# Two attention stages of a three-block layer stack, with heads taken in pairs

## The chip, the cores and the metric

One core of a Trainium2 chip runs the whole program in one launch. The metric is device microseconds for one execution of it. TensorE (PE in the profile), VectorE (DVE), ScalarE (ACT) and the queue of SyncE (SP), which issues the transfers, run side by side and meet at semaphores.

## The reference, cut to what matters

The program computes three transformer-like blocks for 512 tokens of width 1024 in fp32. Two of their pieces are touched, both with 8 heads of width 64:

```python
# block 1: the attention over selected keys (8 heads of 64), queries in 4 blocks of 128
logits = jnp.einsum('bqhd,bqkhd->bqhk', qb, k_sel) * scale
logits = jnp.where(valid[:, :, None, :], logits, -jnp.inf)
p = jax.nn.softmax(logits, axis=-1)
out = jnp.einsum('bqhk,bqkhd->bqhd', p, v_sel)
# block 2: the neighbourhood attention (8 heads of 64), local keys with a bias, and 256 context keys
s_loc = jnp.einsum('brnqhd,brnjwhd->bhrnqjw', qb, k_band) + bias
s_loc = jnp.where(col_valid[:, :, None, :], s_loc, NEG_INF)
s_ctx = jnp.einsum('brnqhd,blhd->bhrnql', qb, kcx)
p = jax.nn.softmax(jnp.concatenate([s_loc, s_ctx], axis=-1), axis=-1)
o = p_loc @ v_band + p_ctx @ vcx
```

The kernel does both densely: the selection of keys and the window are a bias that is added before the softmax.

## The kernel before

The program is a row of stages with a barrier between them. Each stage gives each engine its own list of instructions, written out in Python and never reordered; waits on named counters stand in the lists. `project` (L351) multiplies weight blocks with activations, one tile of 128 output rows after another, and takes other work along in the dictionaries `tensor_beside`, `scalar_beside` and `vector_beside`: a part at key n stands behind tile n, a part at n - 0.5 stands in the middle of tile n on TensorE, and behind tile n - 1 on the two others.

**The selected-key stage** (`dsa_attention`, L1584) runs beside eight such tiles (L454, 8 matmul records of 512 columns each, taken from the bank by VectorE in L1626). **The neighbourhood stage** (`neighbourhood_attention`, L1757) has no tiles: TensorE does attention and two small sums for the normalisation of a convolution (`conv_norm`, L1709), nothing else.

Both use class `Attention` (L1346). Its unit is one head and one block of 128 queries, 32 units a stage. A unit goes through these steps, on one engine after the other:

- scores on TensorE (L1395): one matmul of 64 rows by up to 512 key columns (selected keys: 128, 256, 384 or 512 of them, by the query block), or 512 and 256 columns (neighbourhood). They go to one of two sets of score banks, by turns.
- on VectorE, scale and bias (L1439, counter `softened`) and the row minimum (L1448). In the neighbourhood stage ScalarE scales the 256 context columns (`scale_plain`, L1469, counter `plain_scaled`).
- on ScalarE the exponential with its row sum (L1487), on VectorE the reciprocal (L1454) and the normalisation (L1456).
- on TensorE the transposes (L1410), on ScalarE the copy out of the bank (L1481), on TensorE the products with the values (L1421): a matmul of 128 rows and 64 output columns for each 128 keys, moving 128 columns.

In the neighbourhood stage VectorE adds the window to the bias table of a head before its first unit (L1783), and the queue loads the tables ahead (L1772), two buffers by turns.

The units are staggered. In turn i TensorE does the scores of unit i+1, the transposes of unit i-2 and the values of unit i-3. The scores of unit i wait until unit i-2 has left the same banks. Both operands are fp32, and each fp32 matmul stands in the trace as two records with a weight load each; a transpose is one record.

## Time and profile before

| | |
|---|---|
| median of 3 runs | 3605.81 us (3605.07 to 3607.76) |
| the profiled execution | 3607.01 us, its span 3605.2 us |
| TensorE busy | 3319.2 us, 92% of the span |
| VectorE busy | 1498.6 us, 42% |
| ScalarE busy | 728.0 us, 20% |
| mean granted TensorE clock | 0.964 |

The span is the time between the first and the last instruction in the profile of one execution. A matmul record's length includes the way through the array, so that records which follow each other overlap; what one costs is read from start to start. The granted clock is 1.00 at 2.4 GHz and 0.50 at 1.2 GHz.

### The profile page before, as it was taken

To read this page: it belongs to the slowest core of one execution; us is meant where nothing else is said; L and a number is where in the kernel's file an instruction comes from. 1 tells how busy PE (TensorE), PEld (TensorE's weight loads), DVE (VectorE), ACT (ScalarE), POOL (GpSimd) and SP (SyncE) were. 2 spreads that over 40 slices of the span, in tenths; PEclk is the share of its full clock that TensorE was granted. 3 is DMA by queue.
4 is the path that set the end of the run, shared out by engine and by line. 5 is a ranking of instruction groups with operands and counts; after the bars stand their busy time and mean duration, and the time that the engine had idled before them with its cause. 6 is when DMAs were issued, how large, how long until landed. Compare 5 with 4: busy or idle time off the path is not lost. (4 is left out here: it accounts for less than half of the span.)

```text
span 3605.2 us, 39699 instructions
## 1 busy us (share of the span) xinstructions
PE 3319.2 (92%) x16514; PEld 1917.2 (53%) x16514; DVE 1498.6 (42%) x2289; ACT 728.0 (20%) x1116; POOL 0.2 (0%) x4
## 2 busy tenths in 40 slices
PE   7998999998998969999989898899998999999997
PEld 3485545444455633332323232587554887877874
DVE  2563147611376432212121211436442767466662
ACT  2210232311105310000000000200521323231403
POOL 0000000000000000000000000000000000000000
PEclk9997999999998979999999999999999999999998
DMA  7202042123111049999999999322111212211110
GB/s 254 93 3 71 24 137 103 47 94 140 59 66 36 12 163 387 428 427 428 427 428 428 427 428 427 123 94 88 51 56 61 70 47 70 71 70 47 71 47 24
DMA packets 120306, 588.33 MB, mean 163 GB/s; under 512 B 8896, under 2 KB 11072, under 8 KB 95424
## 3 DMA queue, kind: packets, MB, share of 16 engines
q1 hardware_dynamic: 120128, 585.80, 40.8%
q8 instruction: 131, 2.15, 0.2%
q14 instruction: 47, 0.39, 0.0%
HBM read 583.68 MB, written 2.10 MB: 162 GB/s over the span
## 5 line engine op out<-in xcount | busy, mean ns | idle before, releaser
L454 PE MATMUL ps<-hT,weight_ring 128*128 128x512 f32 x1216 | 544.1, 605 | 28.6 <-ACT hT L593 8.8
L454 PE MATMUL ps<-work,weight_ring 128*128 128x512 f32 (+1 forms) x960 | 425.0, 592 | 18.3 <-PEq L2443 8.3
L454 PEld LDWEIGHTS ps<-hT,weight_ring 128*128 128x128 f32 x1216 | 233.3, 195 | 316.0 <-issue 304.8
L454 PEld LDWEIGHTS ps<-work,weight_ring 128*128 128x128 f32 x960 | 181.0, 194 | 215.6 <-issue 205.0
L2016 PE MATMUL ps<-weight_ring,work 128*64 128x512 f32 x944 | 217.5, 605 | 31.2 <-DMA weight_ring<-in_w_up 17.6
L326 DVE TENSOR_TENSOR work<-work,ps 128x512 f32<-128x512 f32 x196 | 134.7, 687 | 248.7 <-PE ps L441 244.1
L441 PE MATMUL ps<-weight_ring 128*128 128x256 f32 x896 | 202.8, 380 | 0.0
L2145 DVE SCALAR_TENSOR_TENSOR xT<-ps,mod,xT 128x512 f32<-128x512 f32 x128 | 96.1, 751 | 228.3 <-PE ps L2034 225.9
L441 PE MATMUL ps<-hT,weight_ring 128*128 128x256 f32 x704 | 165.4, 393 | 19.5 <-DVE hT L602 15.6
L441 PEld LDWEIGHTS ps<-weight_ring 128*128 128x128 f32 x896 | 170.1, 190 | 24.3 <-issue 1.9
L2016 PE MATMUL ps<-work 128*64 128x512 f32 x688 | 158.2, 603 | 21.6 <-DMA work<-in_w_up 13.5
L441 PE MATMUL ps<-weight_ring,spare_slot 128*128 128x256 f32 x704 | 159.7, 380 | 3.6 <-DVE weight_ring L292 3.6
L2016 PEld LDWEIGHTS ps<-weight_ring,work 128*64 128x64 f32 x944 | 66.2, 138 | 175.9 <-issue 131.3
L441 PEld LDWEIGHTS ps<-hT,weight_ring 128*128 128x128 f32 x704 | 137.3, 197 | 41.6 <-issue 21.8
L441 PEld LDWEIGHTS ps<-weight_ring,spare_slot 128*128 128x128 f32 x704 | 133.4, 190 | 23.3 <-issue 5.8
L1395 PE MATMUL ps<-work 64*128 64x256 f32 (+5 forms) x256 | 106.0, 521 | 20.1 <-DVE work L1439 13.0
L2016 PEld LDWEIGHTS ps<-work 128*64 128x64 f32 x688 | 48.1, 138 | 125.6 <-issue 95.4
L2140 DVE TENSOR_TENSOR work<-work,ps 128x512 f32<-128x512 f32 x32 | 33.9, 1060 | 191.6 <-PE ps L2016 191.0
L2160 DVE COPY work<-ps 128x512 f32<-128x512 f32 x16 | 11.1, 692 | 243.4 <-PE ps L2070 243.4
L545 ACT COPY work<-ps 128x512 f32<-128x512 f32 (+1 forms) x45 | 24.6, 547 | 397.1 <-PE ps L454 208.3
L2070 PE MATMUL ps<-weight_ring,work 128*64 128x512 f32 x448 | 100.2, 595 | 4.0 <-DMA weight_ring<-in_w_down 2.3
L1421 PE MATMUL ps<-work 128*64 128x128 f32 (+1 forms) x704 | 99.8, 285 | 0.0
(346 smaller groups left out, 4169.8 us busy)
## 6 DMA issues: line engine op xcount, KB each, us to landing
weight_ring<-in_w_gate SPq DMA_DIRECT2D x34, 2048.0 KB, 40.2
weight_ring<-in_w_down SPq DMA_DIRECT2D x28, 2048.0 KB, 40.3
weight_ring<-in_w_up SPq DMA_DIRECT2D x25, 2048.0 KB, 38.2
work<-in_w_up SPq DMA_DIRECT2D x23, 2048.0 KB, 38.2
work<-in_w_gate SPq DMA_DIRECT2D x20, 2048.0 KB, 40.2
work<-in_w_down SPq DMA_DIRECT2D x20, 2048.0 KB, 40.3
weight_ring<-in_w_in_odd SPq DMA_DIRECT2D x20, 2048.0 KB, 7.8
weight_ring<-in_w_in SPq DMA_DIRECT2D x18, 2048.0 KB, 9.0
```

The costliest lines, as they stand in the source:

```text
L326: v(dve.tensor_tensor(out, x, got, op), sig if out is steps[-1][0] else None)
L441: ins = pe.matmul(bank[:, j * L:(j + 1) * L], st, mv, start=k == 0, stop=k == 3)
L454: ins = pe.matmul(bank[0:m, 0:f], w[:, k, where:where + m], src[:, k, 0:ntok], start=k == 0, stop=k == kt - 1)
L545: return (lambda a, act, ps, sig: a(act.copy(out, ps), sig), None)
L1395: ins = pe.matmul(self.score_banks(i)[:, c0:c0 + n], u["q"], k, start=True, stop=True)
L1421: ins = pe.matmul(self.ch.ps[u["rows"], self.value_bank + gi % 2, u["col"]:u["col"] + P], val, self.pT[(i - 3) % 2][:, t * P:(t + 1) * P], ...
L2016: ins = pe.matmul(ps[64 * h:64 * h + 64, 1 + 2 * u + n, :], xs[:, 2 * (i % 2) + t, i // 2, :], w[:, t, c0:c0 + 512], start=i == 0 and t == ...
L2070: ins = pe.matmul(ps[64 * q:64 * q + 64, 7, :], hidT[:, i // 2, t, i % 2, :], w[:, t, q * 512:(q + 1) * 512], start=i == 0 and t == 0, sto ...
L2140: v(dve.tensor_tensor(by_tile(hid[:, p, :]), strided(sil[:, p, :]), strided(ps[:, 3 + p, :]), MUL), hid_ready)
L2145: v(dve.scalar_tensor_tensor(ch.xT[:, n, :], ps[:, scatter_banks(e, i // 2)[i % 2], :], ch.mod2[:, 40 + n, 0:1], ch.xT[:, n, :], MUL, ADD) ...
L2160: v(dve.tensor_copy(y, ps[:, 7, :]), y_ready)
```

## The change

A new class `PairAttention` takes the place of `Attention` in the two stages (a third user of `Attention`, in block 3, stays). Its unit is a pair of heads and one block of queries, 16 pairs a stage. The two heads of a pair have their queries and keys in rows 0 to 63 and 64 to 127 of the array, and the score matmuls of the two are written alternately. The values of the two heads go to output columns 0 to 63 and 64 to 127 of one bank, again written alternately. The four sets of banks stay in number: what were two sets of score banks for consecutive units is now one set, half of it for each head of the pair. So the scores of pair i+1 wait until pair i has left the banks. In turn i TensorE does the scores of pair i+1, the transposes of the first head of pair i-2, the values of pair i-3, and the transposes of the second head of pair i-2. Six probability buffers and four for the transposed ones take room in the spare slot. The bias tables have four buffers in the place of `hT`, and VectorE prepares two of them at a time. The convolution's parts stand behind turns 0, 1, 2, 3 and 5 instead of 0, 1, 3, 5 and 8.

```diff
@@ -1494,6 +1494,158 @@
...
+class PairAttention:
+        self.turn_bank, self.value_bank = bank + 2 * width, bank + 3 * width
+        pieces = [x[:, n:n + cols] for x in rooms for n in range(0, SLOT - cols + 1, cols)]
+        self.S, self.pT = pieces[0:6], pieces[6:10]
...
+    def score_banks(self, a):
+        b = self.bank + self.width * a
+        return self.ch.ps[:, b:b + self.width, :].rearrange("p b n -> p (b n)")
...
+    def score(self, pe, i):
+        if i < self.N:
+            u = self.pairs[i]
+            if i >= 1:
+                pe.wait_ge(self.softened.sem, self.softened.at(2 * i))
+                if u["plain"]:
+                    pe.wait_ge(self.plain_scaled.sem, self.plain_scaled.at(2 * i))
+            for c0, n in u["keys"]:
+                for a in range(2):
+                    ins = pe.matmul(self.score_banks(a)[:, c0:c0 + n], u["q"][a], u["k"][a][:, c0:c0 + n], start=True,
+                                    stop=True)
+            ins.then_inc(self.scores.sem, 1)
+            self.scores.total += 1
+    def turn(self, pe, i, a):
+        if 0 <= i < self.N:
+            pe.wait_ge(self.normed.sem, self.normed.at(2 * i + a + 1))
+            if 2 * i + a >= 1:
+                pe.wait_ge(self.copied.sem, self.copied.at(2 * i + a))
+            for t in range(self.pairs[i]["cols"] // P):
+                ins = pe.transpose(self.turn_banks()[:, t * P:(t + 1) * P],
+                                   self.S[2 * (i % 3) + a][:, t * P:(t + 1) * P], self.ch.m("ident"))
+            ins.then_inc(self.turned.sem, 1)
+            self.turned.total += 1
+    def values(self, pe, i):
+        if 0 <= i < self.N:
+            u, g = self.pairs[i], self.group[i]
+            pe.wait_ge(self.copied.sem, self.copied.at(2 * i + 2))
+            if g >= 2:
+                pe.wait_ge(self.taken.sem, self.taken.at(g - 1))
+            n = len(u["v"][0])
+            for t in range(n):
+                for a in range(2):
+                    ins = pe.matmul(self.ch.ps[64 * a:64 * a + 64, self.value_bank + g % 2, u["col"]:u["col"] + P],
+                                    u["v"][a][t], self.pT[2 * (i % 2) + a][:, t * P:(t + 1) * P], start=t == 0,
+                                    stop=t == n - 1)
+            ins.then_inc(self.summed.sem, 1)
+            self.summed.total += 1
+    def tensor(self, i):
+        def part(pe):
+            if i == 0:
+                self.score(pe, 0)
+            self.score(pe, i + 1)
+            self.turn(pe, i - 2, 0)
+            self.values(pe, i - 3)
+            self.turn(pe, i - 2, 1)
+        return part
+    def vector(self, i):
+        def part(v, dve):
+            if i < self.N:
+                u = self.pairs[i]
+                v.after(self.scores, i + 1)
+                if i >= 3:
+                    v.after(self.turned, 2 * (i - 2))
+                if u.get("prepare"):
+                    u["prepare"](v, dve)
+                for a in range(2):
+                    b, w = u["bias"][a], u["biased"]
+                    v(dve.scalar_tensor_tensor(self.S[2 * (i % 3) + a][:, 0:w], self.score_banks(a)[:, 0:w], -self.scale, b,
+                                               MUL, SUB), self.softened)
+                for a in range(2):
+                    if u["plain"]:
+                        v.after(self.plain_scaled, 2 * i + a + 1)
+                    v(dve.tensor_reduce(self.st[:, 2 * (i % 3) + a, 1:2], self.S[2 * (i % 3) + a][:, 0:u["cols"]], AXX, MIN),
+                      self.taken_max)
+            if 1 <= i < self.N + 1:
+                j = i - 1
+                for a in range(2):
+                    stat, x = self.st[:, 2 * (j % 3) + a, :], self.S[2 * (j % 3) + a][:, 0:self.pairs[j]["cols"]]
+                    v.after(self.expd, 2 * j + a + 1)
+                    v(dve.reciprocal(stat[:, 3:4], stat[:, 2:3]))
+                    v(dve.tensor_scalar(x, x, stat[:, 3:4], None, MUL), self.normed)
+            if i >= 5 and self.pairs[i - 5]["close"] is not None:
+                v.after(self.summed, i - 4)
+                self.pairs[i - 5]["close"](v, dve, self.ch.ps[:, self.value_bank + self.group[i - 5] % 2, :], self.taken)
+        return part
+    def scale_plain(self, act_line, act, i):
+        if i < self.N and self.pairs[i]["plain"]:
+            act_line.after(self.scores, i + 1)
+            if i >= 3:
+                act_line.after(self.turned, 2 * (i - 2))
+            c0, w = self.pairs[i]["plain"]
+            for a in range(2):
+                act_line(act.mul(self.S[2 * (i % 3) + a][:, c0:c0 + w], self.score_banks(a)[:, c0:c0 + w], -self.scale),
+                         self.plain_scaled)
+    def scalar(self, i):
+        def part(line, act):
+            if i == 0:
+                self.scale_plain(line, act, 0)
+            for a in range(2):
+                j = i - 2
+                if 0 <= j < self.N:
+                    n = self.pairs[j]["cols"]
+                    line.after(self.turned, 2 * j + a + 1)
+                    if j >= 2:
+                        line.after(self.summed, j - 1)
+                    line(act.copy(self.pT[2 * (j % 2) + a][:, 0:n], self.turn_banks()[:, 0:n]), self.copied)
+                if i < self.N:
+                    x, stat = self.S[2 * (i % 3) + a][:, 0:self.pairs[i]["cols"]], self.st[:, 2 * (i % 3) + a, :]
+                    line.after(self.taken_max, 2 * i + a + 1)
+                    line(act.activation(x, x, ACT.Exp, bias=stat[:, 1:2], scale=-1.0, accum_out=stat[:, 2:3]), self.expd)
+            self.scale_plain(line, act, i + 1)
+        return part
+    def spread(self, beside, places):
+        for i in range(self.turns):
+            beside.add(places[min(i, len(places) - 1)], self.tensor(i), self.scalar(i), self.vector(i))
...
@@ in dsa_attention
...
     q, k, v, gate, bias, out = (ch.slot(9), ch.slot(10), ch.slot(4), ch.slot(3), ch.slot(7), ch.slot(11))
-    units = []
-    for h in range(8):
-        rows, j = slice(64 * (h % 2), 64 * (h % 2) + 64), h // 2
+    pairs, both = [], (slice(0, 64), slice(64, 128))
+    for j in range(4):
         for s in range(4):
             n = P * (s + 1)
             def close(line, dve, ps, sig, j=j):
                 line(dve.tensor_tensor(out[:, j, :], ps, gate[:, j, :], MUL), sig)
-            units.append(dict(
-                q=q[rows, j, s * P:(s + 1) * P], keys=[(k[rows, j, 0:n], 0)],
-                biases=[(bias[:, s, 0:n], 0, n)], plain=[], cols=n,
-                values=[v[:, t, h * HD:(h + 1) * HD] for t in range(s + 1)],
-                rows=rows, col=s * P, close=close if h % 2 == 1 and s == 3 else None))
+            pairs.append(dict(
+                q=[q[rows, j, s * P:(s + 1) * P] for rows in both], k=[k[rows, j, 0:n] for rows in both], keys=[(0, n)],
+                bias=[bias[:, s, 0:n]] * 2, biased=n, plain=None, cols=n,
+                v=[[v[:, t, (2 * j + a) * HD:(2 * j + a + 1) * HD] for t in range(s + 1)] for a in range(2)],
+                col=s * P, close=close if s == 3 else None))
     beside = Beside()
-    att = Attention(ch, units, HD ** -0.5, bank=3, width=1, room=ch.slot(0, 2))
-    att.spread(beside, [-1] * 3 + sorted(halves(0, 8) * 2))
+    att = PairAttention(ch, pairs, HD ** -0.5, 3, 1, [ch.slot(0, 2).rearrange("p k t -> p (k t)"), ch.spare[:, :]], T)
+    att.spread(beside, [-1] * 2 + halves(0, 8))
     beside.project(ch, 2, tiles, banks=3)
@@ in neighbourhood_attention
-    flat = ch.slot(11).rearrange("p a t -> p (a t)")
-    tab = [flat[:, i * 896:(i + 1) * 896] for i in range(2)]
+    flat = ch.hT[:, :, :].rearrange("p k t -> p (k t)")
+    tab = [flat[:, i * 896:(i + 1) * 896] for i in range(4)]
     loaded = ch.counter("bias_loaded")
 
     def load(sp):
         softened = att.softened
         for h in range(8):
-            if h >= 2:
-                sp.wait_ge(softened.sem, softened.at(4 * (h - 1)))
-            sp.dma_start(tab[h % 2], ch.A["rpb"][:, h * 896:(h + 1) * 896]).then_inc(loaded.sem, 16)
+            if h >= 4:
+                sp.wait_ge(softened.sem, softened.at(8 * (h // 2 - 1)))
+            sp.dma_start(tab[h % 4], ch.A["rpb"][:, h * 896:(h + 1) * 896]).then_inc(loaded.sem, 16)
             loaded.total += 16
             sp.wait_ge(loaded.sem, loaded.total)
 
-    units = []
-    for h in range(8):
-        rows, j = slice(64 * (h % 2), 64 * (h % 2) + 64), h // 2
-
-        def prepare(line, dve, h=h):
-            line.after(loaded, 16 * (h + 1))
-            t = tab[h % 2].rearrange("p (r c) -> p r c", c=64)
-            line(dve.tensor_tensor(t, t, ch.m("win")[:, 0:64].unsqueeze(1).to_broadcast([P, 14, 64]), ADD))
+    pairs, both = [], (slice(0, 64), slice(64, 128))
+    for j in range(4):
+        def prepare(line, dve, j=j):
+            for h in (2 * j, 2 * j + 1):
+                line.after(loaded, 16 * (h + 1))
+                t = tab[h % 4].rearrange("p (r c) -> p r c", c=64)
+                line(dve.tensor_tensor(t, t, ch.m("win")[:, 0:64].unsqueeze(1).to_broadcast([P, 14, 64]), ADD))
+        def close(line, dve, ps, sig, j=j):
+            line(dve.tensor_copy(out[:, j, :], ps), sig)
         for s in range(4):
-            def close(line, dve, ps, sig, j=j):
-                line(dve.tensor_copy(out[:, j, :], ps), sig)
-            units.append(dict(
-                q=q[rows, j, s * P:(s + 1) * P], keys=[(k[rows, j, 0:512], 0), (k[rows, j, 512:768], 512)],
-                biases=[(tab[h % 2][:, (6 - 2 * s) * 64:(6 - 2 * s) * 64 + 512], 0, 512)], plain=[(512, 256)],
-                cols=768, values=[v[:, t, h * HD:(h + 1) * HD] for t in range(6)],
-                rows=rows, col=s * P, close=close if h % 2 == 1 and s == 3 else None,
-                prepare=prepare if s == 0 else None))
-    att = Attention(ch, units, HD ** -0.5, bank=0, width=2, room=ch.slot(9, 2))
+            c0 = (6 - 2 * s) * 64
+            pairs.append(dict(
+                q=[q[rows, j, s * P:(s + 1) * P] for rows in both], k=[k[rows, j, :] for rows in both],
+                keys=[(0, 512), (512, 256)], bias=[tab[(2 * j + a) % 4][:, c0:c0 + 512] for a in range(2)], biased=512,
+                plain=(512, 256), cols=768,
+                v=[[v[:, t, (2 * j + a) * HD:(2 * j + a + 1) * HD] for t in range(6)] for a in range(2)],
+                col=s * P, close=close if s == 3 else None, prepare=prepare if s == 0 else None))
+    att = PairAttention(ch, pairs, HD ** -0.5, 0, 2, [ch.slot(9, 2).rearrange("p k t -> p (k t)"), ch.spare[:, :]], 768)
     (total, square_total), (square, take_root, finish), (centre, scale), made = conv_norm(
         ch, y, ch.slot(5), ch.slot(6), 7)
 
     def conv_made(pe):
         pe.wait_ge(made.sem, made.at(4))
-    convolution = {0: (total, None, centre), 1: (None, square, None), 3: (square_total, take_root, scale),
-                   5: (None, finish, None), 8: (conv_made, None, None)}
+    convolution = {0: (total, None, centre), 1: (None, square, None), 2: (square_total, take_root, scale),
+                   3: (None, finish, None), 5: (conv_made, None, None)}
     beside = Beside()
     for i in range(att.turns):
         beside.add(-1, att.tensor(i), att.scalar(i), att.vector(i))
```

**The neighbourhood stage, TensorE.** The list of one turn in its middle, before (L1395 scores, L1410 transposes, L1421 values; one unit):

```order
L1395 MATMUL ps<-work 128x512 [waits plain_scaled,scores_scaled]
L1395 MATMUL ps<-work 128x256
L1410 MATMUL ps<-masks,work 128x128 [waits probs_copied,probs_normed]
L1410 MATMUL ps<-masks,work 128x128 x5
L1421 MATMUL ps<-work 64x128 [waits probs_copied]
L1421 MATMUL ps<-work 64x128 x5
```

The same list after, one turn again, which is two heads (L1542 scores, L1553 transposes, L1567 values):

```order
L1542 MATMUL ps<-work 128x512 [waits plain_scaled,scores_scaled]
L1542 MATMUL ps<-work 128x512
L1542 MATMUL ps<-work 128x256 x2
L1553 MATMUL ps<-masks,work 128x128 [waits probs_copied,probs_normed]
L1553 MATMUL ps<-masks,work 128x128 x5
L1567 MATMUL ps<-spare_slot,work 64x128 [waits probs_copied]
L1567 MATMUL ps<-spare_slot,work 64x128 x11
L1553 MATMUL ps<-masks,spare_slot 128x128 [waits probs_copied,probs_normed]
L1553 MATMUL ps<-masks,spare_slot 128x128 x5
```

The number of matmuls for a head is as before; the matmuls of the two heads now stand next to each other, and the second head's transposes stand behind the values.

**The neighbourhood stage, ScalarE.** One turn before (L1481 the copy of transposed probabilities, L1487 the exponential, L1469 the context columns of the next unit):

```order
L1481 COPY work<-ps 128x768 [waits values_summed,probs_turned,plain_scaled]
L1487 ACTIVATE work,small<-work,small 128x768 [waits maxima_ready,probs_copied]
L1469 ACTIVATE work<-ps 128x256 [waits probs_turned,scores,exps_done]
```

And one turn after (L1635 the copy, L1639 the exponential, L1621 the context columns of the next pair):

```order
L1635 COPY spare_slot<-ps 128x768 [waits values_summed,probs_turned,plain_scaled]
L1639 ACTIVATE work,small<-work,small 128x768 [waits maxima_ready,probs_copied]
L1635 COPY spare_slot<-ps 128x768 [waits values_summed,probs_turned,exps_done]
L1639 ACTIVATE spare_slot,small<-spare_slot,small 128x768 [waits maxima_ready,probs_copied]
L1621 ACTIVATE work<-ps 128x256 [waits probs_turned,scores,exps_done]
L1621 ACTIVATE work<-ps 128x256 [waits plain_scaled]
```

The context columns of both heads of the next pair now stand behind the copy and the exponential of the second head.

**The selected-key stage, VectorE.** The list from the end of a tile on, after (L1777 takes the tile's bank, L1594 is scale and bias, L1599 the minimum, L1606 and L1607 the normalisation):

```order
L1777 TENSOR_TENSOR work<-ps,work 128x512 [waits tile_ready,probs_normed]
L1594 SCALAR_TENSOR_TENSOR work<-ps,work 128x512 [waits probs_turned,scores,tile_vector_done]
L1594 SCALAR_TENSOR_TENSOR work<-ps,work 128x512 [waits scores_scaled]
L1599 TENSOR_REDUCE small<-work 128x1 [waits scores_scaled]
L1599 TENSOR_REDUCE small<-work 128x1 [waits maxima_ready]
L1606 RECIPROCAL small<-small 128x1 [waits exps_done,maxima_ready]
L1607 TENSOR_SCALAR work<-work,small 128x384 [waits vector_step]
```

The pair's scale and bias stand behind the tile's L1777, as a unit's stood before; TensorE's next scores, right behind the tile's last matmul in its list, now wait for these two L1594 instead of for those of a unit earlier.

## Rows read from the trace of the kernel before

**Rows 1.** Windows of the stages: us, then busy (x records) by engine, clock, DMA, GB/s.

```profile
638.00:731.00 93.00, 92.62 (x366) 47.05 (x367) 56.50 (x139) 35.84 (x97) 0.00 (x0) 0.95 0.09 30
1077.00:1231.00 154.00, 140.71 (x720) 93.99 (x720) 95.47 (x149) 84.22 (x143) 0.00 (x0) 0.89 0.12 38
1150.00:1220.00 70.00, 70.00 (x410) 48.25 (x410) 52.59 (x84) 40.88 (x76) 0.00 (x0) 1.00 0.07 21
```

**Rows 2.** Timeline of TensorE, neighbourhood stage: start us, length us, operation.

```profile
1138.77 1.55 PE L1395 MATMUL ps<-work 64*128 64x512 f32 x4
1140.25 0.88 PE L1410 MATMUL ps<-masks,work 128*128 128x128 f32 x6
1141.06 1.52 PE L1421 MATMUL ps<-work 128*64 128x128 f32 x12
1142.51 1.55 PE L1395 MATMUL ps<-work 64*128 64x512 f32 x4
```

**Rows 3.** Timeline of ScalarE and VectorE, neighbourhood stage.

```profile
1130.14 0.93 ACT L1487 ACTIVATE work<-work,small 128x768 f32<-128x768 f32 x1
...
1131.20 0.38 ACT L1469 ACTIVATE work<-ps 128x256 f32<-128x256 f32 x1
...
1131.68 0.95 DVE L1448 TENSOR_REDUCE small<-work 128x1 f32<-128x768 f32 x1 [2.91 <-ACT work L1469]
```

**Rows 4.** Groups by line, 1130 to 1225 us: busy us, mean ns, idle before.

```profile
L1448 DVE TENSOR_REDUCE small<-work 128x1 f32<-128x768 f32 x25 | 23.8, 953 | 23.4 <-ACT work L1469 23.0
...
L1481 ACT COPY work<-ps 128x768 f32<-128x768 f32 x25 | 20.0, 799 | 36.0 <-PE ps L1410 36.0
...
L1439 DVE SCALAR_TENSOR_TENSOR work<-ps,work 128x512 f32<-128x512 f32 x24 | 16.6, 692 | 0.8
...
L1783 DVE TENSOR_TENSOR work<-work,masks 128x896 f32<-128x896 f32 x6 | 6.6, 1093 | 0.5 <-PE ps L1410 0.4
```

**Rows 5.** Timeline of TensorE where other stages alternate halves or quarters.

```profile
205.54 3.73 PE L1007 MATMUL ps<-work 64*64 64x128 f32 x128 [2.22 <-PEq L936]
...
1357.14 5.38 PE L2016 MATMUL ps<-weight_ring,work 128*64 128x512 f32 x24
...
1459.19 1.13 PE L2034 MATMUL ps<-work 64*128 64x512 f32 x4
```

**Rows 6.** Timeline of TensorE behind pauses; the pause stands in brackets.

```profile
1086.42 1.80 PE L1395 MATMUL ps<-work 64*128 64x512 f32 x4 [2.72 <-DVE work L1439]
...
1116.48 2.92 PE L1395 MATMUL ps<-work 64*128 64x512 f32 x4 [5.14 <-DVE work L1439]
...
2835.21 4.96 PE L441 MATMUL ps<-spare_slot,weight_ring 128*128 128x256 f32 x14 [2.40 <-DVE work L326]
...
3007.64 3.72 PE L441 MATMUL ps<-spare_slot,weight_ring 128*128 128x256 f32 x16 [2.40 <-DVE work L326]
```

**Rows 7.** Windows behind such pauses; the clock is third from the end.

```profile
2835.00:2838.50 3.50, 3.29 (x8) 2.67 (x9) 3.39 (x4) 0.83 (x2) 0.00 (x0) 0.53 0.40 147
...
3007.00:3011.00 4.00, 3.36 (x16) 2.98 (x17) 3.89 (x4) 0.91 (x2) 0.00 (x0) 1.00 0.48 178
1087.60:1104.60 17.00, 13.46 (x36) 7.86 (x35) 10.54 (x17) 10.88 (x19) 0.00 (x0) 0.50 0.10 28
```

**Rows 8.** The bias tables (L1772) and timeline of the start-up.

```profile
DMA to landing us min/median/max: 3.3/3.6/7.3
...
1084.55 1.09 DVE L1783 TENSOR_TENSOR work<-work,masks 128x896 f32<-128x896 f32 x1 [20.03 <-DMA work<-in_rpb]
...
1130.63 2.20 PE L1395 MATMUL ps<-work 64*128 64x512 f32 x4
```

**Rows 9.** Timeline of TensorE over one tile, and a group of VectorE, selected-key stage.

```profile
700.97 1.99 PE L454 MATMUL ps<-work,weight_ring 128*128 128x512 f32 x4
702.88 0.48 PE L1395 MATMUL ps<-work 64*128 64x128 f32 x2
...
712.18 0.70 PE L454 MATMUL ps<-work,weight_ring 128*128 128x512 f32 x1
...
L1626 DVE TENSOR_TENSOR work<-ps,work 128x512 f32<-128x512 f32 x8 | 5.5, 692 | 13.3 <-PE ps L454 13.3
```

More of the change, by code:

```diff
@@ L1494, in spread, with __init__, turn_banks @@
             beside.add(places[min(n, len(places) - 1)], self.tensor(i), self.scalar(i), self.vector(i))
+class PairAttention:
+    def __init__(self, ch, pairs, scale, bank, width, rooms, cols):
+        self.ch, self.pairs, self.scale, self.width, self.bank = ch, pairs, scale, width, bank
+        self.turn_bank, self.value_bank = bank + 2 * width, bank + 3 * width
+        pieces = [x[:, n:n + cols] for x in rooms for n in range(0, SLOT - cols + 1, cols)]
+        self.S, self.pT = pieces[0:6], pieces[6:10]
+        self.st = ch.sm[:, 96:120].rearrange("p (i c) -> p i c", c=4)
+        (self.scores, self.softened, self.taken_max, self.expd, self.normed, self.turned, self.copied,
+         self.summed, self.taken, self.plain_scaled) = ch.counters(
+            "scores", "scores_scaled", "maxima_ready", "exps_done", "probs_normed", "probs_turned",
+            "probs_copied", "values_summed", "group_taken", "plain_scaled")
+        self.N = len(pairs)
+        self.turns = self.N + 5
+        self.group, g = [], 0
+        for u in pairs:
+            self.group.append(g)
+            g += u["close"] is not None
+    def score_banks(self, a):
+        b = self.bank + self.width * a
+        return self.ch.ps[:, b:b + self.width, :].rearrange("p b n -> p (b n)")
+    def turn_banks(self):
+        return self.ch.ps[:, self.turn_bank:self.turn_bank + self.width, :].rearrange("p b n -> p (b n)")
+    def score(self, pe, i):
[103 more added lines that the diff above has]
+            beside.add(places[min(i, len(places) - 1)], self.tensor(i), self.scalar(i), self.vector(i))
```

## The prediction

> **What bounds the two stages now.** I read the windows first. The two stages are 93 and 154 us of the 3605.2 us span, and TensorE is busy for nearly all of the first and for all of the middle of the second [rows 1]. Nothing outside them is edited, so the change moves the time by what these 247 us gain or lose, and what follows is made of transfers and products that start when the stage ends.
>
> Then the timeline. In the middle of the neighbourhood stage one unit takes 1142.51 - 1138.77 = 3.74 us: 1.48 for the scores, 0.81 for six transposes, 1.45 for the values, from start to start, with no pause [rows 2]. So TensorE bounds it, at 7.49 us for the two heads of what will be a pair. VectorE is busy 52.59 of 70 us there, which is 5.6 us per pair, and ScalarE 40.88 of 70, 4.4 us per pair [rows 1]. They wait for TensorE and for each other: the copy waits for the transposes, 36.0 us in all, and the row minimum for the context columns from ScalarE, 23.0 us [rows 4].
>
> **Do the halves run together?** The new class itself is not in the trace, but other stages alternate halves. In column halves, 24 records of 512 columns take 5.38 us, 0.22 us each [rows 5]; the score stage shows what one such record costs alone: two of 512 and two of 256 columns in 1.48 us [rows 2], about 0.43. In row halves, four records of 512 columns are over in 1.13 us [rows 5], where one after another they would need 1.7. With 128 columns in quarters a record costs 3.73/128 = 0.03 us [rows 5], against 1.45/12 = 0.12 in the value stage [rows 2]. So I take both halvings as given: a pair's scores 1.48, its values 1.46, its transposes 2 x 0.81. TensorE's own work for a pair falls from 7.49 to 4.56 us in the neighbourhood stage.
>
> **What becomes late: the neighbourhood stage.** The scores of pair i+1 now wait for pair i to leave the only set of banks, and the context columns of pair i are the last thing in ScalarE's turn, behind the copy and the exponential of the second head. The copy waits for the second head's transposes, and these stand at the end of TensorE's turn. This closes a loop. Once round: scores 1.48, transposes 0.81, values 1.45, transposes to their end 0.88 [rows 2]; a semaphore, about 0.1 (the minimum begins 0.10 us behind the end of the context columns, 1131.68 against 1131.20 + 0.38) [rows 3]; the copy 0.80 and 0.03 to the next instruction [rows 4]; from the exponential to the context columns 1131.20 - 1130.14 = 1.06 [rows 3]; two sets of context columns 0.38 + 0.41 [rows 3]; a semaphore 0.1. The sum is 7.5 us for a pair, where TensorE alone needed 7.49. All that the halves save goes into a pause of 7.5 - 4.6 = 2.9 us in front of the scores. VectorE's way round is shorter (two L1439, 1.45 us, where ScalarE needs 2.8), except where it prepares tables: two L1783 of 1.1 us [rows 4] stand in front of the two L1439, and 3.7 us take the place of 2.8. That adds 1.0 us at three pairs; before, it was hidden under TensorE.
>
> The sum at full clock: the twelve pairs of the middle, 0; the tables, +3; the last pair's way through copy, transposes and values with nothing beside it, two heads instead of one, +3.5 (an estimate: one more transpose stage, copy and semaphores). At the start the second table has to land too: it is issued when the first has landed, just before 1084.55, and takes 3.6 us [rows 8]. The first subtraction then begins some 3.5 us later. Against this, eight units used to need 1130.63 - 1077.0 = 53.6 us until the ninth unit's scores [rows 1, 8], with pauses of 2.72 and 5.14 us [rows 6] and 17 us at half clock [rows 7]; VectorE's list for the same eight now goes in four turns with fewer waits between. I take -5 with the late table in it. Together +1.5 us.
>
> **What the pause does to the clock.** In this stage before, a pause of 2.72 us was followed by the granted clock at 0.50 for 17 us, from 1087.6 on [rows 6, 7], and scores cost twice as much: 2.92 us for the four records behind the pause of 5.14 [rows 6]. Elsewhere a pause of 2.40 us was followed by 0.53 for 3.5 us at 2835, and an equal one at 3007 by no fall [rows 6, 7]. A pause of 2.9 us in each of twelve turns lies between these, nearer to the one that did fall. I take three in four of them to be followed by 3.5 us at half clock. TensorE is on the loop in that stretch, so each costs half of it, 1.7 us: 12 x 0.75 x 1.7 = +15. The bounds are 0, and every turn's TensorE work at half clock, 12 x 4.6 = +55. Neighbourhood stage: +16.5.
>
> **The selected-key stage.** One tile with four units takes 712.18 - 700.97 = 11.2 us, of which the two halves of the tile are 2 x 1.91 = 3.8 [rows 9] and ten transposes in four groups some 1.7 (from 0.81 for six [rows 2]). The rest, 5.7, is scores and values, and halves to 2.85. So a tile with its two pairs has 8.4 us of work on TensorE. New is the wait at a tile's end: the scores there need the two L1594 of the pair before, which stand in VectorE's list behind the eviction of that very tile. That is a semaphore, 0.7 for the eviction [rows 9], two of up to 0.7 [rows 4], a semaphore: 2.4 us where the pair is 512 keys wide, and an estimated 1.9 at 256. With 0.2 for the second head's transposes behind the first's copy, a tile comes to 10.7 us, 0.5 less than before, -4 for eight. Four of these waits are 2.4 us long, as the pauses at 2835 and 3007 were; I take two falls, 2 x 1.7 = +3.5. The stage comes out at -0.5 (from -5 to +5).
>
> **Sum.** +16.5 - 0.5 = +16, made against the profiled 3607.01 us (span 3605.2), which gives 3623; the median of the runs shown is 1.2 us lower, so 3622.
>
> **The rivals.**
>
> *The clock holds.* The pauses are there, but TensorE's denser work on either side of them (both row halves at once) keeps the clock up, as behind the pause at 3007. Then +1.5 and -4 are left: 3603. The fall at 1087.6 speaks against it.
>
> *The copying engines bound it, not the loop (faster).* If the waits overlapped better than I lay out, the neighbourhood stage would run at VectorE's busy time, 5.6 us for a pair: 12 x (7.5 - 5.6) = -23, and with no pause over 2 us no falls: 3607 + 1.5 - 23 - 4 - 1 = 3580. It decides from the point where the scores of the next pair can start before ScalarE has gone through the second head. For it speaks that no engine is full; against it, the list of ScalarE, in which the context columns stand last. The Trainium skill (TensorEngine Tiling (Array Packing), PSUM Bottleneck) says that tiling makes TensorE faster but not the emptying of PSUM, which may then bound, and advises to use both ScalarE and VectorE for it. By that rule alone the stage would gain; here both engines are used, and the trace shows their busy time well under the loop.
>
> *Half clock throughout.* If each fall lasts as in this stage before, 17 us, the clock does not come back between two pauses: +55 instead of +15, and +5 in the other stage: 3667; half of the way there, 3645.
>
> *The halves don't run together* (the change doesn't do what it says): the loop grows by 1.4 + 1.4 us for twelve pairs, +34, and eight tiles by 5.7 - 2.85 each, +23; some 3675. The rates of the other stages speak against it [rows 5].
>
> **How the numbers follow.** The forecast has 0.65, with a range of its own from 3610 to 3640 (6 to 14 falls, the start at -8 to 0). The clock holds: 0.13. The copying engines bound it: 0.09. Half clock throughout or most of the way: 0.10. No overlap: 0.03. The range from 3600 to 3646 holds the first two and part of the fourth, 0.8. A measurement of this kernel can tell about 0.2%, 7.2 us, from no change. Faster than 3598.6 is only the copying engines' case, with the edge of the held clock, 0.10; within the bound are the rest of the held clock and the low edge of the forecast, 0.17; slower 0.73.
>
> **What the profile after would show.** In the neighbourhood stage: scores of a pair at 1.5 us for eight records, values at 1.5 for 24; a turn of 7.5 us at full clock; a pause of 2.9 us in front of L1542, put down to ScalarE's L1621; a granted clock clearly under 0.89 over the stage; 170 us instead of 154. In the selected-key stage: pauses of about 2.3 us in front of every second L1542, released by VectorE L1594, and 93 us as before. The prediction is wrong if the pause is much shorter than 2.9 us, if the clock stays at 1.00 through it, or if the turn is not bound by the loop.

## The result, and the profile after

The changed kernel takes 3621.6 us (median of 5 runs, 3618.82 to 3624.95) against 3605.81 us: ratio 1.0042, 95% interval 1.0029 to 1.0056. It is slower by 15.8 us. The profiled execution took 3624.95 us, span 3623.1 us, against a span of 3605.2 us before.

The windows of the changed kernel, the stages first, then a stretch at half clock and one at full clock (us, busy time and records by engine as in [rows 1], clock, DMA share, GB/s):

```profile
638.00:731.00 93.00, 70.44 (x368) 34.21 (x368) 60.23 (x147) 35.89 (x97) 0.00 (x0) 0.93 0.16 56
1077.00:1249.00 172.00, 101.86 (x720) 66.62 (x720) 94.95 (x149) 84.45 (x144) 0.00 (x0) 0.82 0.11 34
...
1156.80:1159.90 3.10, 3.10 (x20) 2.15 (x18) 1.87 (x5) 0.82 (x2) 0.00 (x0) 0.50 0.00 0
1160.40:1173.40 13.00, 6.16 (x64) 4.46 (x61) 8.55 (x13) 7.52 (x15) 0.00 (x0) 1.00 0.24 71
```

Read the PE column first. In the neighbourhood stage TensorE's busy time fell from 140.71 to 101.86 us [rows 1], so the halves do run together; and yet the stage grew from about 153 us to 171 (first score record to last value record), because nearly 70 us of it are now pauses. The granted clock fell from 0.89 to 0.82. With two levels, a mean of 0.82 over 172 us is 2 x 0.18 x 172 = 62 us at half clock, against 2 x 0.11 x 154 = 34 before.

TensorE's timeline of the changed kernel: four waits at a tile's end in the selected-key stage, the scores of pairs 5 to 16 of the neighbourhood stage with what stands between two of them, and the stage's end.

```profile
657.49 0.49 PE L1542 MATMUL ps<-work 64*128 64x128 f32 x4 [2.30 <-DVE work L1594]
...
659.41 3.07 PE L454 MATMUL ps<-work,weight_ring 128*128 128x512 f32 x4
...
679.59 0.49 PE L1542 MATMUL ps<-work 64*128 64x128 f32 x4 [2.30 <-DVE work L1594]
...
700.29 0.49 PE L1542 MATMUL ps<-work 64*128 64x128 f32 x4 [2.30 <-DVE work L1594]
...
709.70 0.92 PE L1542 MATMUL ps<-work 64*128 64x384 f32 x4 [1.77 <-DVE work L1594]
...
1126.54 2.93 PE L1542 MATMUL ps<-work 64*128 64x512 f32 x8 [8.48 <-DVE work L1594]
1136.47 2.93 PE L1542 MATMUL ps<-work 64*128 64x512 f32 x8 [3.93 <-DVE work L1594]
1146.43 2.92 PE L1542 MATMUL ps<-work 64*128 64x512 f32 x8 [3.82 <-ACT spare_slot L1621]
1155.61 1.88 PE L1542 MATMUL ps<-work 64*128 64x512 f32 x8 [2.92 <-ACT work L1621]
1164.73 1.56 PE L1542 MATMUL ps<-work 64*128 64x512 f32 x8 [2.92 <-ACT work L1621]
1166.22 0.88 PE L1553 MATMUL ps<-masks,work 128*128 128x128 f32 x6
1167.03 1.53 PE L1567 MATMUL ps<-spare_slot,work 128*64 128x128 f32 x24
1168.49 0.87 PE L1553 MATMUL ps<-masks,spare_slot 128*128 128x128 f32 x6
1173.29 2.48 PE L1542 MATMUL ps<-work 64*128 64x512 f32 x8 [3.93 <-DVE spare_slot L1594]
1182.42 1.56 PE L1542 MATMUL ps<-work 64*128 64x512 f32 x8 [2.92 <-ACT work L1621]
1189.97 2.10 PE L1542 MATMUL ps<-work 64*128 64x512 f32 x8 [2.92 <-ACT work L1621]
1199.10 1.56 PE L1542 MATMUL ps<-work 64*128 64x512 f32 x8 [2.92 <-ACT spare_slot L1621]
1207.65 2.71 PE L1542 MATMUL ps<-work 64*128 64x512 f32 x8 [3.93 <-DVE work L1594]
1216.84 1.67 PE L1542 MATMUL ps<-work 64*128 64x512 f32 x8 [2.92 <-ACT work L1621]
1225.95 2.93 PE L1542 MATMUL ps<-work 64*128 64x512 f32 x8 [2.92 <-ACT spare_slot L1621]
...
1247.17 1.53 PE L1567 MATMUL ps<-spare_slot,work 128*64 128x128 f32 x24 [0.93 <-ACT spare_slot L1635]
```

Eight score records for two heads take 1.49 us from start to start (1166.22 - 1164.73), where four for one head took 1.48; 24 value records 1.46, where 12 took 1.45 [rows 2]. Then comes the pause. Its releaser is ScalarE's L1621, and VectorE's L1594 at the pairs whose tables are prepared. Both engines of the changed kernel from the pair at 1161 on, and VectorE at the start of the stage:

```profile
1088.41 1.09 DVE L1933 TENSOR_TENSOR hT<-hT,masks 128x896 f32<-128x896 f32 x1 [2.33 <-DMA hT<-in_rpb]
1089.53 1.42 DVE L1594 SCALAR_TENSOR_TENSOR work<-ps,hT 128x512 f32<-128x512 f32 x2
...
1161.89 0.80 ACT L1635 COPY spare_slot<-ps 128x768 f32<-128x768 f32 x1 [0.99 <-ACT work L1639]
1162.73 0.94 ACT L1639 ACTIVATE work<-work,small 128x768 f32<-128x768 f32 x1
...
1163.79 0.80 ACT L1621 ACTIVATE work<-ps 128x256 f32<-128x256 f32 x2
...
1169.57 2.22 DVE L1933 TENSOR_TENSOR hT<-hT,masks 128x896 f32<-128x896 f32 x2 [1.65 <-PE ps L1553]
1171.82 0.69 DVE L1594 SCALAR_TENSOR_TENSOR work<-ps,hT 128x512 f32<-128x512 f32 x1
```

The copy begins when the second head's transposes are out, at 1161.89; the exponential and both context columns end at 1164.59; the scores start at 1164.73. That is the loop, with the members that the prediction named. At 1169.57 the two tables stand in front of the two L1594, and the pause is 3.93 us instead of 2.92.

### The profile page after: what moved, and what is told of

It reads as the page before. It is cut to its first block and busy times, and to the rows that moved or that the text cites. A ratio compares the mean times of both kernels' runs of the same rounds, so it can differ in the third digit from the quotient of the medians.

```text
span 3623.1 us, 39618 instructions
## 1 busy us (share of the span) xinstructions
PE 3262.4 (90%) x16514; PEld 1877.1 (52%) x16514; DVE 1498.8 (41%) x2289; ACT 728.9 (20%) x1116; POOL 0.2 (0%) x4
## 5 line engine op out<-in xcount | busy, mean ns | idle before, releaser
L2168 PE MATMUL ps<-work 128*64 128x512 f32 x688 | 156.5, 597 | 20.0 <-DMA work<-in_w_up 13.3
L1542 PE MATMUL ps<-work 64*128 64x256 f32 (+3 forms) x192 | 52.3, 662 | 84.5 <-DVE work L1594 47.4
L2473 DVE TENSOR_TENSOR xT<-ps,xT 128x512 f32<-128x512 f32 x48 | 33.2, 692 | 158.2 <-PE ps L454 158.1
```

Source lines behind the costliest of these rows:

```text
L1542: ins = pe.matmul(self.score_banks(a)[:, c0:c0 + n], u["q"][a], u["k"][a][:, c0:c0 + n], start=True, stop=True)
L2168: ins = pe.matmul(ps[64 * h:64 * h + 64, 1 + 2 * u + n, :], xs[:, 2 * (i % 2) + t, i // 2, :], w[:, t, c0:c0 + 512], start=i == 0 and t == ...
L2473: v(dve.tensor_tensor(ch.xT[:, n, :], ps, ch.xT[:, n, :], ADD), sig)
```

## The experiments

Each is the changed kernel with one edit. Ratios are against the kernel before, timed on the same chip in the same rounds (3606.95 us in the batch of the first four told here, which were run together; 3605.91 in that of the others). The changed kernel was not timed again in these batches. A difference from it is one of medians from different batches; counted from each batch's kernel before, it is up to 1.1 us larger.

### The two stages apart

`e3_selected_only`: the function `neighbourhood_attention` is that of before, `dsa_attention` that of after. `e4_neighbourhood_only` is the opposite.

> Pairs in the selected-key stage alone; the neighbourhood stage is that of the kernel before. Theory (the whole loss is in the neighbourhood stage): the selected-key stage takes about 90 us instead of 93, the program about 3603 us, ratio to before 0.998 to 1.000. Rival (the new waits of 2.3 and 1.8 us in front of the scores at each tile's end cost more than the halves save): this stage loses, 3608 us or more.

> Pairs in the neighbourhood stage alone; the selected-key stage is that of the kernel before. Theory: the stage takes 170 to 173 us instead of 154, the program about 3624 us, ratio 1.0045 to 1.006. Rival (the loss is in the selected-key stage): 3606 us, ratio 1.000.

Pairs in the selected-key stage alone: 3598.93 us, ratio 0.9979 (0.9970 to 0.9987), 8.0 us faster. Pairs in the neighbourhood stage alone: 3630.68 us, ratio 1.0069 (1.0052 to 1.0086), 23.7 us slower. The two add up to +15.7, the whole change's +15.8; the intervals are some 3 and 6 us to either side, so that the sum could have missed by several us. The gain is larger than was expected (3603 us), and so is the loss (3624 us). So the edit has a gain and a loss, and the loss sits in the neighbourhood stage. The windows of that stage in the second one:

```profile
1077.00:1255.00 178.00, 108.89 (x720) 72.18 (x720) 94.72 (x148) 84.28 (x143) 0.00 (x0) 0.77 0.10 33
```

Its code is the changed kernel's, but the clock is 0.77 instead of 0.82, 82 us at half clock instead of 62, and the stage is 6.6 us longer. The same lists can thus lose more or less to the clock. The stage begins at 1077.28 us here and at 1077.61 in the changed kernel, and what makes the difference the record doesn't show; the runs of this kernel spread from 3621.56 to 3641.97.

### Does the pause lower the clock?

`e1_values_twice` fills a part of the pause with work that nobody needs: in the neighbourhood stage the 24 value records of a pair are computed a second time behind the second head's transposes, and ScalarE's and VectorE's lists are untouched. The output stays what it was; the signal that the values are summed goes out behind the second time.

```diff
-            self.values(pe, i - 3)
+            self.values(pe, i - 3, self.width == 1)
             self.turn(pe, i - 2, 1)
+            if self.width == 2:
+                self.values(pe, i - 3)
```

> The changed kernel with each pair's value products of the neighbourhood stage done a second time, behind the second head's transposes, so that 1.46 us of the pause of 2.9 us in front of the scores are filled with work that nobody needs and that makes nobody wait. Output unchanged. Theory (each pause lets the clock fall, and the falls cost some 15 us): the pauses shrink to 1.5 us, no falls in the middle of the stage, the turn stays at 7.5 us, the stage shortens by 8 to 14 us, the program to 3608 to 3614 us although TensorE does 16 x 1.46 us more. Rival (the clock's falls cost nothing because TensorE waits anyway): 3622 us or more.

3614.97 us, ratio 1.0023 (1.0014 to 1.0032), just above the 3608 to 3614 us expected: 384 records more, and 6.6 us less than the changed kernel. The slowest of its nine runs, 3617.80 us, is under the fastest of the changed kernel, 3618.82. Its window:

```profile
1160.00:1220.00 60.00, 46.34 (x527) 35.26 (x524) 42.36 (x66) 35.01 (x64) 0.00 (x0) 1.00 0.06 17
```

Its timeline of TensorE:

```profile
1157.16 1.56 PE L1542 MATMUL ps<-work 64*128 64x512 f32 x8 [1.46 <-ACT work L1624]
...
1164.71 1.56 PE L1542 MATMUL ps<-work 64*128 64x512 f32 x8 [1.46 <-ACT work L1624]
...
1173.27 1.56 PE L1542 MATMUL ps<-work 64*128 64x512 f32 x8 [2.46 <-DVE spare_slot L1597]
```

The pause is 1.46 us, shorter by just the added work. The clock is 1.00 where the changed kernel had 0.90 over the same 60 us. And the turn is 1164.71 - 1157.16 = 7.55 us although TensorE has 6.1 us of work in it, not 4.6: its own work does not set the turn. Of the eleven turns from pair 5 to pair 16 the first three are still longer than at full clock, by 5.5 us together, where the changed kernel has eight and 13.3 us; the stage takes 162.8 us instead of 171.1. This shows two things apart, that the loop bounds the turn and that the pause costs clock on top of it.

### Is it ScalarE's list that closes the loop?

`e2_context_first` puts the next pair's context columns ahead of the second head's copy and exponential.

```diff
             for a in range(2):
                 j = i - 2
+                if a == 1:
+                    self.scale_plain(line, act, i + 1)
...
-            self.scale_plain(line, act, i + 1)
```

> The changed kernel with ScalarE's context columns of the next pair moved ahead of the second head's copy and exponential. Nothing else. Theory (the turn is the loop scores, transposes, values, transposes, copy, exponential, context columns): the loop loses copy and exponential, 1.9 us, and VectorE becomes the bound at 5.7 to 6.2 us a turn; 12 to 15 turns by 1.5 us and most of the falls: 3600 to 3607 us. Rival (the turn is bound by VectorE or by the transposes alone): the turn stays at 7.5 us, 3622 us.

3599.63 us, ratio 0.9982 (0.9973 to 0.9991), 22 us less than the changed kernel. Its timeline:

```profile
1151.28 1.56 PE L1542 MATMUL ps<-work 64*128 64x512 f32 x8 [1.66 <-DVE work L1594]
...
1155.03 0.88 PE L1553 MATMUL ps<-masks,work 128*128 128x128 f32 x6
...
1156.04 1.42 DVE L1594 SCALAR_TENSOR_TENSOR work<-ps,hT 128x512 f32<-128x512 f32 x2 [1.19 <-PE ps L1553]
...
1157.51 1.56 PE L1542 MATMUL ps<-work 64*128 64x512 f32 x8 [1.60 <-DVE work L1594]
```

The turn is 6.23 us. Now the other way round the loop ends last: VectorE's L1594 also waits for the second head's transposes, and its two take 1.42 us where ScalarE's three steps took 2.8. In the middle of the stage no pause over 2 us is left except at the tables. There it is still 3.92 us, the turn still 8.56, and a fall of the clock follows both times (1166.07 and 1194.92). The mean clock of the stage rises to 0.87, and it takes 151.2 us.

### Is it TensorE's list?

`e5_scores_last` leaves ScalarE and VectorE alone and moves the scores to the end of TensorE's turn.

```diff
-            self.score(pe, i + 1)
             self.turn(pe, i - 2, 0)
             self.values(pe, i - 3)
             self.turn(pe, i - 2, 1)
+            self.score(pe, i + 1)
```

> The changed kernel with the scores of pair i+1 written behind the second transposes in each turn, in both stages, instead of at the turn's head. Theory (the scores' wait is what holds up the transposes and values behind it in TensorE's list): at a tile's end the transposes and values fill the wait of 2.3 us, the selected-key stage falls to 81 to 85 us; in the neighbourhood stage transposes and values run under ScalarE's copy and exponential, the turn falls to 5.7 to 6.3 us, the stage to 140 to 150 us, with few falls of the clock; the program about 3580 to 3592 us. Rival (only ScalarE's order counts, the scores' place doesn't): 3615 us or more.

3580.02 us, ratio 0.9927 (0.9913 to 0.994): 26 us faster than the kernel before, 42 us faster than the changed one. Its window in the neighbourhood stage:

```profile
1130.00:1190.00 60.00, 48.50 (x468) 34.08 (x464) 56.90 (x91) 46.30 (x84) 0.00 (x0) 1.00 0.06 16
```

Its timeline of TensorE and VectorE, a wait at a tile's end of the selected-key stage first:

```profile
689.93 0.49 PE L1542 MATMUL ps<-work 64*128 64x128 f32 x4 [1.08 <-DVE work L1594]
...
1152.22 1.42 DVE L1594 SCALAR_TENSOR_TENSOR work<-ps,hT 128x512 f32<-128x512 f32 x2
...
1153.59 0.84 PE L1553 MATMUL ps<-masks,work 128*128 128x128 f32 x6 [0.42 <-ACT spare_slot L1635]
...
1154.37 1.56 PE L1542 MATMUL ps<-work 64*128 64x512 f32 x8
...
1157.36 1.42 DVE L1594 SCALAR_TENSOR_TENSOR work<-ps,hT 128x512 f32<-128x512 f32 x2
```

The scores still wait for the same two engines, but the next turn's transposes and values now stand ahead of that wait instead of behind it: 3.1 us of TensorE's work are done while ScalarE and VectorE empty the banks. One turn here is 1157.36 - 1152.22 = 5.14 us, which is one of the short ones: the nine turns between the scores at 1131.89 and at 1183.74 last 4.8 to 6.5 us, 5.76 in the mean, with two tables' preparations in them. VectorE is busy 56.90 of 60 us, the clock stays at 1.00, and the stage takes some 138 us. The selected-key stage, which has no context columns, also gains: its waits at a tile's end fall from 2.30 to about 1.1 us, and it takes 78 us instead of 88. This kernel is what the rival "the copying engines bound it" described, 3580 us.

`e8_last_and_tables` adds the edit of `e7_two_tables_at_once` below to it.

> The scores behind the second transposes and the two tables at once, together. If both gains stand on their own: 1.5 to 3.5 us under the kernel with the scores last alone, 3578 to 3590 us, which is under both kernels. Rival (the start is bound by the convolution's chain, not by the table): equal to it.

3579.08 us, ratio 0.9922 (0.9909 to 0.9936), not to be told from `e5_scores_last`.

### Are the halves concurrent because they alternate?

`e6_heads_one_by_one` issues first all matmuls of one head, then those of the other, in scores and in values.

```diff
-            for c0, n in u["keys"]:
-                for a in range(2):
+            for a in range(2):
+                for c0, n in u["keys"]:
...
-            for t in range(n):
-                for a in range(2):
+            for a in range(2):
+                for t in range(n):
```

> The changed kernel with the matmuls of the two heads written one head after the other (all scores of the first, then of the second; likewise the values) instead of alternately. Theory (halves run together only where they stand next to each other in the list): only the last record of one head meets the first of the other; a pair's scores take about 2.3 to 2.5 us instead of 1.5 and its values 2.6 to 2.8 instead of 1.5 where 768 keys wide, the loop grows by some 2 us, 3650 to 3670 us. Rival (TensorE looks far enough ahead to run them together, or order plays no part because of the pause): 3622 us.

3645.84 us, ratio 1.0111 (1.0097 to 1.0124). Its timeline of TensorE:

```profile
1086.64 1.57 PE L1542 MATMUL ps<-work 64*128 64x512 f32 x8 [1.14 <-PEq L394]
...
1157.92 2.18 PE L1542 MATMUL ps<-work 64*128 64x512 f32 x8 [2.92 <-ACT spare_slot L1621]
...
1167.98 2.00 PE L1542 MATMUL ps<-work 64*128 64x512 f32 x8 [2.92 <-ACT work L1621]
1169.91 1.54 PE L1553 MATMUL ps<-masks,work 128*128 128x128 f32 x6
...
1230.43 2.94 PE L1542 MATMUL ps<-work 64*128 64x512 f32 x8 [3.93 <-DVE work L1594]
1233.30 1.12 PE L1553 MATMUL ps<-masks,work 128*128 128x128 f32 x6
...
1259.62 2.45 PE L1567 MATMUL ps<-spare_slot,work 128*64 128x128 f32 x24
1262.01 0.87 PE L1553 MATMUL ps<-masks,work 128*128 128x128 f32 x6
```

Only lengths at one level of the clock can be compared. The values take 1262.01 - 1259.62 = 2.4 us instead of 1.46, at a granted clock of 1.00 in both kernels; one head after the other with nothing shared would be 2.9. The scores lose nothing: the stage's first pair, at clock 1.00, is 1.57 us long against 1.56 in the changed kernel, and at clock 0.50 a pair takes 1233.30 - 1230.43 = 2.87 us, where the changed kernel has 1129.40 - 1126.54 = 2.86. The 1.93 us from 1167.98 on have a fall of the clock in them (mean 0.76 from 1167.9 to 1170.0).

So the order of the records gives most of the concurrency in the values, where the other head's records now stand 12 places off, and none in the scores, where they stand 4 places off. The values of the selected-key stage, column halves too, tell that it goes by the distance. At clock 1.00 and 4 places off, 8 records are 0.66 us long, as alternated; 6 places off, 12 records are 1.14 us long against 0.88; 8 places off, 16 records 1.58 against 1.09 (665.54, 671.76 and 676.46 in this trace; 663.52, 669.74 and 674.22 in the changed kernel's). For the scores the rival came true, and the 3650 us or more that were expected did not come out. The pause is 2.92 us as before, and the loop got longer by the 0.9 us of its values. A turn is 1167.98 - 1157.92 = 10.06 us: 7.55, these 0.9, and 1.6 for a fall of the clock, which all eleven turns have here and eight have in the changed kernel. The selected-key stage takes 96 us instead of 88.

### Is the second table late?

`e7_two_tables_at_once` issues the first two tables without a wait between them.

```diff
             loaded.total += 16
-            sp.wait_ge(loaded.sem, loaded.total)
+            if h:
+                sp.wait_ge(loaded.sem, loaded.total)
...
-                line.after(loaded, 16 * (h + 1))
+                line.after(loaded, 32 * (j + 1))
```

> The changed kernel with the first two bias tables issued without a wait between, and VectorE waiting for both before it prepares either. Theory (the late second table costs the start of the neighbourhood stage 3.5 us): VectorE starts both additions some 9 to 10 us after the stage's start instead of 11 to 12 for the second, the program is 1.5 to 3.5 us shorter than the changed kernel. Rival (something else is late at the start, or the two transfers share the rate): 0.

3622.0 us, ratio 1.0043 (1.0031 to 1.0056): no gain over the changed kernel's 1.0042, a miss. VectorE at the start of its stage:

```profile
1083.20 2.22 DVE L1934 TENSOR_TENSOR hT<-hT,masks 128x896 f32<-128x896 f32 x2 [21.23 <-DMA hT<-in_rpb]
1085.45 1.42 DVE L1594 SCALAR_TENSOR_TENSOR work<-ps,hT 128x512 f32<-128x512 f32 x2
...
1094.81 0.69 DVE L1882 TENSOR_SCALAR work<-ps 128x512 f32<-128x512 f32 x1 [5.97 <-PE ps L1869]
```

Here L1934 is the preparation, and both tables are there before the first of the two starts; the first L1594 begins 10.7 us behind the stage's first scores (1074.72), where the changed kernel had 1089.53 - 1077.61 = 11.9. Only 1.2 us of the 3.5 that I had put on this wait can be had in this way, since two tables sent at once land later than one. And 0.5 of that goes into the next wait, for the convolution's sum on TensorE (5.97 us instead of 5.44).

## Why the prediction was right

It said 3622 us, and 3621.6 came out, by the mechanism forecast. That the number agrees to within 1 us is luck: measured alone, the two stages are worth -8.0 and +23.7 us, where the forecast has -0.5 and +16.5, two misses of some 7 us that cancel. The steps one by one, for the profiled execution:

- **Halves run together**: pair's scores 1.49 us (forecast 1.48), values 1.46 (1.46). Right.
- **The loop**: forecast 7.5 us a turn at full clock with a pause of 2.9 in front of L1542, released by ScalarE. Measured 1189.97 - 1182.42 = 7.55, with 2.92. Right. `e1_values_twice` loads TensorE's list without making the turn longer, and `e2_context_first` and `e5_scores_last` open the loop on ScalarE's and on TensorE's side; each turns out as the account says.
- **Tables**: forecast +1.0 at three pairs; turns 8.56 us (1164.73 to 1173.29) against 7.55. Right.
- **The start**: forecast -5. From the first scores to those of pair 5, 1126.54 - 1077.61 = 48.9 us. Before it was 53.4, from the first scores at 1077.25 (the prediction's 53.6 counts from the window's start): -4.5. The sum was right. The first subtraction does begin 3.5 us later, 11.9 us behind the first scores against 8.4 before (1085.67 - 1077.25); how much of that the stage pays was not measured, since `e7_two_tables_at_once` takes only 1.2 us of it away.
- **The stage's end**: forecast +3.5. From the last pair's scores to the last value record, 22.8 us; before, from the next to last unit's scores, 16.3 us by these two rows of the kernel before:

```profile
1213.65 1.55 PE L1395 MATMUL ps<-work 64*128 64x512 f32 x4
...
1227.14 2.83 PE L1421 MATMUL ps<-work 128*64 128x128 f32 x24
```

  That is +6.4, of which 2.8 are a fall of the clock (the pair's scores 2.93 us long instead of 1.56, one transpose stage and one value stage likewise), so +3.6 at full clock. Right.
- **The clock**: forecast three falls in four pauses, 1.7 us each, +15. The eleven turns from pair 5 to pair 16 last 9.93, 9.96, 9.18, 9.12, 8.56, 9.13, 7.55, 9.13, 8.55, 9.19 and 9.11 us. Against 7.55 (8.55 with tables) eight of them are longer, most by 1.6 us, 13.3 us in all; with the 2.8 at the end, 16.1. Right in share and in size, but the share was a judgement within bounds of 0 and +55, and it is not the same for all pauses. Of the twelve in front of the scores of pairs 5 to 16, the five of 3.82 to 8.48 us all came with half clock in or right behind them, the seven of 2.92 us in four cases. The same eleven turns of `e4_neighbourhood_only`, with the same code in this stage, lose 21.6 us. The Trainium skill (TensorE: Matmul & The Clock Gate, A second HAM failure mode: psum-queue depth-cycling) describes something like it for a bf16 kernel that cycles through its PSUM banks: small pauses between groups of matmuls let the clock swing between its levels. This trace agrees, with 8 of 11 turns.
- **Neighbourhood stage**: -4.5 + 3.1 + 13.3 + 6.4 = +18.3 (3.1 is 11 turns at full clock with tables, 86.1 us, less the 83.0 from 1130.63 to 1213.65 before [rows 8]). Forecast +16.5.
- **Selected-key stage**: forecast -0.5, from a tile of 10.7 us and two falls. Measured 88.5 us from the first score record to the end of the last value record against 93.3, -4.8; alone (`e3_selected_only`) -8.0 for the whole kernel. This is the term that was mis-sized. Two tiles take 700.29 - 679.59 = 20.7 us, a tile 10.35: the waits are 2.30 and 1.77 us where I had 2.4 and 1.9, and TensorE's own work was counted 0.1 to 0.2 too long. And only one of the three pauses of 2.30 us was followed by a fall, the one before 657.49: half a weight tile at 659.41 takes 3.07 us instead of the 1.9 of [rows 9].
- **The rest**: +18.3 - 4.8 is 13.5, and the span grew by 17.9. The selected-key stage began 3.8 us later than before (641.96 against 638.15), behind code that is the same in both kernels; between the two stages 1.4 us were lost, and 0.8 won behind them. Single executions differ by as much elsewhere: in the traces of the ten kernels this stage begins between 638.0 and 644.0 us.

Two slips in the prediction's own sums change nothing: the start's 53.6 us, named above, and the rival without concurrency, whose terms give 3622 + 34 + 23 = 3679 us and not 3675.

`e3_selected_only` gains 3 us more than its stage shows. Its trace has a part of the answer: the neighbourhood stage, with the code of the kernel before, takes 148.1 us there instead of 152.7, with 20.5 us at half clock instead of 34. That is one execution of each.

What stays open: why the clock falls behind some pauses and not behind others of the same length (2.92 us before 1164.73, 1182.42 and 1199.10 without one, before 1155.61, 1189.97, 1216.84 and 1225.95 with one).

## What to carry to other kernels

When matmuls are packed into halves, count how often the banks come free as well as how fast TensorE fills them: with one set of banks, everything that stands behind the waiting matmul in TensorE's list joins the loop, and the gain of the halves turns into a pause. Put the matmul that waits at the end of the turn, behind work that is ready; here one moved line turned a loss of 16 us into a gain of 26. And a recurring pause of 2 to 3 us can cost twice, once as time and once as clock: in the changed kernel a fall followed one of three pauses of 2.30 us, and four of seven of 2.92.

## What was not expected of the hardware

- Useless work made the kernel faster: 384 more records, 6.6 us less, since the clock stayed at 1.00 with pauses of 1.46 us and did not with pauses of 2.92.
- The concurrency of column halves hangs on how far apart the records stand: 24 records take 1.46 us alternated, and 2.4 us with the other half's records 12 places off. With 4 places between them nothing was lost, in column halves (0.66 us for 8 records) or in row halves (1.57 us for 8 against 1.56); with 6 places 12 records were 1.14 us long against 0.88.
- Two transfers of 448 KB issued together made the pair ready only about 1.2 us sooner than one after the other.
